# Three quarters of the sigmoid gates by seven half-block products, with the weight sums on GpSimd

## The chip, the cores and the metric

One core of one Trainium2 chip runs the whole kernel in one launch. The metric is the device time of an execution in microseconds (us), lower is better. Engines are named as in the profile: PE is TensorE, ACT is ScalarE, DVE is VectorE, POOL is GpSimd, SP is SyncE.

## The reference

Two transformer blocks in float32 on 512 tokens of width 1024. What matters here lies in the first block, behind its two attentions ya and yb (each 512 wide):

```
h = rms_norm(x, g_pre[l]);  proj = h @ w_in[l];  ..., gates = split(proj)      # gates: 2048 columns
gate_a, gate_b = split(sigmoid(gates))                                          # 1024 columns each
merged = gate_a * (ya @ w_branch[l, 0]) + gate_b * (yb @ w_branch[l, 1])
y = merged @ w_out[l];  x = x + rms_norm(y, g_post[l])
```

## The kernel before, in words

**Arithmetic.** Every float32 operand of a matrix product is split into a rounded part `hi` and a rest `lo`, and each product is three matmuls, hi·hi, hi·lo and lo·hi (`three`, L1015 to L1019). Activations are held with features on the partitions: `h_hi` and `h_lo` have 8 blocks of 128 features by 512 tokens.

**The ring of weights.** Weights come in halves of 128 x 1024 elements (512 KB). SP loads a half into one of two buffers `w_raw` (`load_half`, L725), ACT copies it rounded into `w_hi` (`split_hi`, L1667), DVE writes the rest `w_lo` (`split_lo`, L2413), and PE uses it. `w_hi` and `w_lo` have four slots; the split of half u waits until PE has done with half u-4 (`slot_free`), and the load of a half waits until the half two before it is split (`split_done`).

**The gates stage.** It follows the second attention ("diff"). The 1024 merged features are done in four quarters of 256. A quarter has four gate halves (128 gate columns each: two of branch A, two of branch B; `gate_group`, L1092, 24 matmuls of 512 columns each) and two branch halves (`branch_half`, L1126, again 24 matmuls each, 12 for ya and 12 for yb). The results go to the four banks of `lin`. ACT applies the sigmoid (L1987, into `t_g`) and splits the weights that come next, DVE multiplies the branch products by the gates (L2723), adds them (`t_c`, L2726) and writes the rest `m_lo` (L2730) beside ACT's `m_hi` (L1992). The two banks of `sc` and the two of `tr` are idle in this stage. Behind it stands the output product `out1` (L1423). Each engine runs its instructions in the order in which they are written; only semaphores tie the engines together.

POOL's work ahead of this stage is the normalising of the attention's rows (`normalise`, L837); in the stage it only issues two loads of gains (L944, L945).

## Time and profile before

| | |
|---|---|
| median of 3 runs | 1180.98 us (1180.74 to 1181.24) |
| the profiled execution, its own time | 1180.78 us |
| span of its trace | 1179.0 us |
| PE busy | 1159.6 us, 98% of the span |
| DVE, ACT, POOL busy | 63%, 53%, 14% |
| granted TensorE clock, mean | 0.998 |

The span runs from the first to the last instruction; the time has 1.8 us more around it. A busy share is an average over all stages, so what a change of one stage is worth is read from that stage's own rows.

### The profile page before, as it was taken

The numbers are of one execution on the slowest core, as the hardware profiler recorded it, in microseconds if no ns is written. First come the engines' busy times: TensorE is split into PE (matmuls) and PEld (weight loads), VectorE is DVE, ScalarE is ACT, GpSimd is POOL, SyncE is SP. The second block draws the span as 40 slices with busy tenths as digits, with TensorE's granted clock in tenths as the row PEclk, the third lists the DMA queues.
The fourth block names the chain that finished last, engine by engine and source line by source line (L and its number), as shares of the span: only waits on it lengthen the run. The fifth ranks groups of instructions, "written<-read, shape, count | busy, mean of one in ns | idle before, by whom it ended". The sixth has DMA issues, their size and how long they took to land.

```text
span 1179.0 us, 15978 instructions
## 1 busy us (share of the span) xinstructions
PE 1159.6 (98%) x5903; PEld 972.7 (83%) x5903; DVE 744.1 (63%) x1227; ACT 625.3 (53%) x1054; POOL 162.5 (14%) x253
## 2 busy tenths in 40 slices
PE   8999999899999999999999999999999999999997
PEld 7788888788888888787878898888988888888885
DVE  6667578754343386684498774464658559568578
ACT  5567786684333255533776453452465355464464
POOL 3244225400000020000133000110010000010010
PEclk9999999999999999999999999999999999999999
DMA  6422232215333552552013555131294562834632
GB/s 201 109 63 64 72 107 72 54 54 143 93 85 107 178 165 75 185 162 77 22 56 125 170 152 154 59 108 56 86 253 106 185 152 58 252 89 102 200 72 89
DMA packets 152170, 136.00 MB, mean 115 GB/s; under 512 B 5569, under 2 KB 122385, under 8 KB 152098
## 3 DMA queue, kind: packets, MB, share of 16 engines
q1 hardware_dynamic: 144688, 113.13, 31.8%
q0 software_dynamic: 4000, 13.67, 6.0%
q10 hardware_dynamic: 3410, 8.25, 1.9%
q8 instruction: 45, 0.74, 0.3%
q14 instruction: 27, 0.22, 0.1%
HBM read 118.20 MB, written 6.82 MB: 106 GB/s over the span
## 4 chain that ended last, share of the span: by engine, by line
PE 86%; DVE 7%; ACT 2%; issue 2%; DMA 2%; POOL 0%; DVEq 0%; ACTq 0%; POOLq 0%
PE lin L1017 23%; PE lin L1019 22%; PE lin L1018 22%; PE tr L1199 2%; PE sc L1019 2%; PE sc L1018 2%; PE sc L1017 2%; PE tr L1192 1%; DVE w_lo L2413 1%; PE tr L1019 1%; PE tr L1018 1%; PE tr L1017 1%; PE sc L1212 1%; PE sc L1209 1%; PE lin L1233 1%
## 5 line engine op out<-in xcount | busy, mean ns | idle before, releaser
L1017 PE MATMUL lin<-h_hi,w_hi 128*128 128x512 f32 (+1 forms) x824 | 316.4, 384 | 0.9 <-ACT g_v L1757 0.7
L1019 PE MATMUL lin<-h_hi,w_lo 128*128 128x512 f32 (+1 forms) x824 | 309.4, 375 | 0.0
L1018 PE MATMUL lin<-h_lo,w_hi 128*128 128x512 f32 (+1 forms) x824 | 309.1, 375 | 0.0
L2413 DVE TENSOR_TENSOR w_lo<-w_raw,w_hi 128x1024 fp32r<-128x1024 f32 x160 | 196.2, 1230 | 136.9 <-ACT w_hi L1667 136.1
L1667 ACT ACTIVATE w_hi<-w_raw 128x1024 fp32r<-128x1024 f32 x162 | 170.6, 1055 | 142.6 <-PE lin L1019 44.5
L1019 PEld LDWEIGHTS lin<-h_hi,w_lo 128*128 128x128 f32 x824 | 155.1, 188 | 28.5
L1017 PEld LDWEIGHTS lin<-h_hi,w_hi 128*128 128x128 f32 x824 | 155.3, 188 | 28.1 <-ACT g_v L1757 0.9
L1018 PEld LDWEIGHTS lin<-h_lo,w_hi 128*128 128x128 f32 x824 | 155.4, 189 | 24.9
L2413 DVE TENSOR_TENSOR u_lo<-u_raw,u_hi 128x256 fp32r<-128x256 f32 (+2 forms) x48 | 37.4, 779 | 70.2 <-ACT u_hi L2297 37.6
L1017 PE MATMUL lin<-w_hi,h_hi 128*128 128x512 f32 x160 | 64.0, 400 | 0.0
L1019 PE MATMUL lin<-w_hi,h_lo 128*128 128x512 f32 x160 | 62.4, 390 | 0.0
L1018 PE MATMUL lin<-w_lo,h_hi 128*128 128x512 f32 x160 | 62.4, 390 | 0.0
L1705 ACT ACTIVATE p<-p,neg_max 128x128 f32<-128x128 f32 (+1 forms) x80 | 44.8, 560 | 33.0 <-DVE neg_max L2444 32.5
L837 POOL TENSOR_SCALAR p<-p,rden 128x128 f32<-128x128 f32 (+1 forms) x80 | 47.3, 592 | 93.9 <-DVE rden L2449 93.5
L2292 ACT ACTIVATE u_raw<-lin 128x512 f32<-128x512 f32 x32 | 19.1, 596 | 71.9 <-PE lin L1019 71.9
L2274 ACT ACTIVATE w_hi<-wd_b 128x1024 fp32r<-128x1024 f32 x32 | 33.5, 1058 | 30.2 <-PE lin L1019 20.4
L1714 ACT ACTIVATE pt_hi<-tr 128x128 fp32r<-128x128 f32 (+1 forms) x80 | 34.3, 429 | 20.0 <-PE tr L1199 19.5
L2454 DVE TENSOR_TENSOR pt_lo<-tr,pt_hi 128x128 fp32r<-128x128 f32 (+1 forms) x80 | 38.5, 484 | 9.0 <-ACT pt_hi L1714 8.5
L2413 DVE TENSOR_TENSOR w_lo<-wd_b,w_hi 128x1024 fp32r<-128x1024 f32 x32 | 38.8, 1224 | 5.2 <-ACT w_hi L2274 5.2
L1199 PE MATMUL tr<-ident,p 128*128 128x128 f32 x200 | 35.6, 276 | 5.6 <-DVE pt_lo L2454 4.5
L2444 DVE CUSTOM_DVE_ANT_0 p<-sc,bias_c 128x128 f32<-128x128 f32 (+3 forms) x52 | 25.3, 487 | 24.3 <-PE sc L1212 22.7
L1017 PE MATMUL sc<-w_hi,u_hi 128*128 128x512 f32 x96 | 37.4, 390 | 0.0
(401 smaller groups left out, 2338.1 us busy)
## 6 DMA issues: line engine op xcount, KB each, us to landing
w_raw<-in_w_in SPq DMA_DIRECT2D x74, 512.0 KB, 4.0
w_raw<-in_w_up SPq DMA_DIRECT2D x32, 512.0 KB, 4.3
wd_b<-in_w_down SPq DMA_DIRECT2D x24, 512.0 KB, 5.2
w_raw<-in_w_out SPq DMA_DIRECT2D x16, 512.0 KB, 3.7
w_raw<-in_w_xkv SPq DMA_DIRECT2D x16, 512.0 KB, 3.9
x_m<-in_x SPq DMA_DIRECT2D x8, 512.0 KB, 6.3
w_raw<-in_w_branch SPq DMA_DIRECT2D x8, 512.0 KB, 3.6
w_raw<-in_w_xq SPq DMA_DIRECT2D x8, 512.0 KB, 3.6
```

The costliest lines, as they stand in the source:

```text
L837: pool.tensor_scalar(p, p, rden[:, s:s + 1], 1.0, ALU.mult, ALU.mult).then_inc(s_norm, 1)
L1017: pe.matmul(o, lh, rh, start=start, stop=False)
L1018: pe.matmul(o, lh, rl, start=False, stop=False)
L1019: return pe.matmul(o, ll, rh, start=False, stop=stop)
L1199: mm = pe.transpose(tr[:, r % 2, P * j:P * j + P], src(j), ident[:, :])
L1667: act.activation(w_hi[u % SLOTS][:, :], w_raw_of(u)[:, :], ACT.Copy).then_inc(w_hi_s, 1)
L1705: act.activation(p, x, ACT.Exp, bias=neg_max[:, s:s + 1], scale=sign, accum_out=denom[:, s:s + 1]).then_inc(s_exp, 1)
L1714: act.activation(blocks(B["pt_hi"], h % 2, i), tr[:, r % 2, 0:P * (i + 1)].rearrange("p (j c) -> p j c", c=P), ACT.Copy)\
L2274: act.activation(w_hi[u % SLOTS][:, :], wd(place, part), ACT.Copy).then_inc(w_hi_s, 1)
L2413: return dve.tensor_tensor(out, x, as_f32(hi), ALU.subtract)
L2444: dve.tensor_tensor_reduce(p, sc[:, s % 2, 0:n], bias[:, T - n:T], -1.0, 3.0e38, ALU.add, ALU.min, neg_max[:, s:s + 1]).then_inc(s_max, 1)
L2454: dve.tensor_tensor(blocks(B["pt_lo"], h % 2, i), tr[:, r % 2, 0:P * (i + 1)].rearrange("p (j c) -> p j c", c=P), as_f32(blocks(B["pt_hi"] ...
```

## The change

The first quarter of the gates stays. In the other three quarters the two gate halves of a branch form a **pair**. Its two by two blocks are the two column blocks by the two halves of the 1024 inputs (4 blocks of 128 each), the tokens are cut into two halves of 256, and the two by two product is computed by seven products of half blocks in place of eight (`gate_pair`): each is 12 matmuls of 256 columns. There are six pairs.

- **Input sums.** Four sums of half blocks of h are made once by POOL (ten additions of 128 x 1024), from the moment the last scores of the attention are done, split by ACT and DVE, and kept.
- **Weight sums.** For each pair POOL makes four sums of 128 x 512 from the two raw halves (`weight_sums`). They are split like weights, two to a slot, so a pair takes four slots: the first half, two sums, the used part of the second half, two sums. Both `w_raw` buffers stay taken until the four sums are made.
- **Products** land in quarters of the ring `sc`, `sc`, `tr`, `tr` (256 columns each). ACT copies products 1 and 6 out, DVE and POOL add up the four quarters of the result, and ACT applies the sigmoid in place.
- The loops over half of the gates, written with register offsets before, are written out.

```
+PAIR_FIRST, PAIR_SUMS_A, PAIR_SECOND, PAIR_SUMS_B = range(4)
+PAIR_ORDER = [1, 2, 4, 3, 5, 6, 7]
...
+        for part, raw, last in ((PAIR_FIRST, True, 2), (PAIR_SUMS_A, False, 4), (PAIR_SECOND, True, 5),
+                                (PAIR_SUMS_B, False, 7)):
+            self.part_of[len(self.half_last_step)] = (pair, part)
+            self.half(name, raw=raw)
+            self.half_last_step[-1] = first + last
...
-    for _ in range(4):
-        p.t_halves("gates", "A", 4)
+    for quarter in range(4):
+        if quarter == 0:
+            p.t_halves("gates", "A", 4)
+        else:
+            p.pair_products("gates")
+            p.pair_products("gates")
...
+            n = 7 * pair + PAIR_ORDER.index(product)
+            return (sc, tr)[n // 2 % 2][:, n % 2, 0:256]
...
+                    if OF_RAW[r - 2] in PLAN.part_of:
+                        sp.wait_ge(gate_sums, 4 * PLAN.part_of[OF_RAW[r - 2]][0] + 4)
...
+            pool.wait_ge(s_done, S0["diff"] + 32)
+            raw = [B["t_raw"][:, n, :, :] for n in range(4)]
+            def of_h(part, row, col):
+                return as_f32(h_block(part, row, col))
+            def h_sum(out, tmp, one, other):
+                link(pool.tensor_tensor(out, of_h("hi", *one), of_h("hi", *other), ALU.add))
+                link(pool.tensor_tensor(tmp, of_h("lo", *one), of_h("lo", *other), ALU.add))
+                pool.tensor_tensor(out, out, tmp, ALU.add).then_inc(turn_made, 1)
+            def h_added(out, x, block):
+                link(pool.tensor_tensor(out, x, of_h("hi", *block), ALU.add))
+                pool.tensor_tensor(out, out, of_h("lo", *block), ALU.add).then_inc(turn_made, 1)
+            h_sum(raw[0], raw[1], (0, 0), (0, 1))
+            pool.wait_ge(turn_made, 1)
+            h_added(raw[1], raw[0], (1, 1))
+            pool.wait_ge(turn_made, 2)
+            h_added(raw[2], raw[1], (1, 0))
+            pool.wait_ge(turn_lo, 1)
+            h_sum(raw[3], raw[0], (0, 1), (1, 1))
             pool.wait_ge(y_lo_s, 8)
             pool.dma_start(B["gain"][:, 0, :], row("g_post")).then_inc(gain_in[1], 16)
             pool.dma_start(B["gain"][:, 1, :], row("norm_mix_2")).then_inc(gain_in[2], 16)
...
+            def weight_sums(pair):
+                u = PAIR_HALF[pair]
+                raw_ready(pool, u)
+                raw_ready(pool, u + PAIR_SECOND)
+                if pair > 0:
+                    split_done(pool, PAIR_HALF[pair - 1] + PAIR_SUMS_B)
+                first, second = w_raw_of(u), w_raw_of(u + PAIR_SECOND)
+                w11, w12, w21, w22 = first[:, 0:T], first[:, T:2 * T], second[:, 0:T], second[:, T:2 * T]
+                s2, s3, s1, s4 = (B["s_raw"][:, n, :] for n in range(4))
+                pool.tensor_tensor(s3, w11, w21, ALU.add).then_inc(gate_sums, 1)
+                pool.wait_ge(gate_sums, 4 * pair + 1)
+                pool.tensor_tensor(s2, s3, w22, ALU.subtract).then_inc(gate_sums, 1)
+                pool.wait_ge(gate_sums, 4 * pair + 2)
+                pool.tensor_tensor(s1, w21, w22, ALU.subtract).then_inc(gate_sums, 1)
+                pool.wait_ge(gate_sums, 4 * pair + 3)
+                pool.tensor_tensor(s4, s2, w12, ALU.subtract).then_inc(gate_sums, 1)
+                pool.wait_ge(gate_sums, 4 * pair + 4)
...
+                pool.wait_ge(gate_copied, 2 * pair + 2)
+                pool.wait_ge(gate_out, 5 * pair + 2)
+                pool.wait_ge(dve_evac, DN[branch_groups(pair // 2, 1) + 1])
+                pool.tensor_tensor(g[:, 0, :], u2, m6, ALU.add).then_inc(gate_rest, 1)
+                pool.wait_ge(gate_out, 5 * pair + 3)
+                pool.tensor_tensor(g[:, 1, :], u3, m6, ALU.add).then_inc(gate_rest, 1)
+            weight_sums(0)
+            for pair in range(0, PAIRS, 2):
+                weight_sums(pair + 1)
+                sums_with_m6(pair)
+                sums_with_m6(pair + 1)
+                if pair + 2 < PAIRS:
+                    weight_sums(pair + 2)
...
+                for k in range(4):
+                    mm = three(pair_place(pair, product), wh[:, k0 + k, :], wl[:, k0 + k, :], xh[:, k, :], xl[:, k, :],
+                               k == 0, k == 3)
...
+            def gate_pair(pair):
+                last = pair - 1
+                if pair > 0:
+                    pe.wait_ge(gate_out, 5 * last + 3)
+                pair_product(pair, 1, PAIR_FIRST, 0, lambda part: h_block(part, 0, 0))
+                if pair > 0:
+                    pe.wait_ge(gate_out, 5 * last + 4)
+                pair_product(pair, 2, PAIR_FIRST, 4, lambda part: h_block(part, 1, 0))
+                if pair > 0:
+                    pe.wait_ge(gate_copied, 2 * last + 2)
+                pair_product(pair, 4, PAIR_SUMS_A, 0, sum_ready(pair, 4))
+                if pair > 0:
+                    pe.wait_ge(gate_out, 5 * last + 5)
+                pair_product(pair, 3, PAIR_SUMS_A, 4, sum_ready(pair, 3))
+                pe.wait_ge(gate_copied, 2 * pair + 1)
+                pair_product(pair, 5, PAIR_SECOND, 4, sum_ready(pair, 5))
+                pe.wait_ge(gate_out, 5 * pair + 1)
+                pair_product(pair, 6, PAIR_SUMS_B, 0, sum_ready(pair, 6))
+                pe.wait_ge(gate_out, 5 * pair + 2)
+                pair_product(pair, 7, PAIR_SUMS_B, 4, lambda part: h_block(part, 1, 1))
...
+                    sums = B["s_raw"][:, 0:2, :] if part == PAIR_SUMS_A else B["s_raw"][:, 2:4, :]
+                    out, x = w_hi[u % SLOTS][:, :], sums.rearrange("p a b -> p (a b)")
+                    act.wait_ge(gate_sums, 4 * pair + (2 if part == PAIR_SUMS_A else 4))
...
+            def pair_copies(pair, behind):
+                u = PAIR_HALF[pair] + SLOTS
+                if pair > 0:
+                    act.wait_ge(gate_out, 5 * (pair - 1) + 2)
+                gate_copy(pair, 1, 0)
+                behind()
+                for part in (PAIR_FIRST, PAIR_SUMS_A, PAIR_SECOND):
+                    split_hi(u + part)
+                if pair > 0:
+                    act.wait_ge(gate_rest, 2 * pair)
+                gate_copy(pair, 6, 1)
...
+            def behind_pair(pair):
+                def f():
+                    split_hi(PAIR_HALF[pair] + SLOTS + PAIR_SUMS_B)
+                    pair_sigmoids(pair)
+                return f
+            for quarter in range(1, 4):
+                first = 2 * quarter - 2
+                pair_copies(first, behind_branches(quarter - 1))
+                pair_copies(first + 1, behind_pair(first))
+                pair_sigmoids(first + 1)
+                split_hi(PAIR_HALF[first + 1] + SLOTS + PAIR_SUMS_B)
+                split_hi(gate_halves(quarter)[1][0] + SLOTS)
+                for n in range(2):
+                    merged_hi(2 * quarter + n)
...
+                pair_done(dve, pair, 2)
+                dve.wait_ge(gate_copied, 2 * pair + 1)
+                dve.tensor_tensor(g[:, 0, 0:256], m1, pair_place(pair, 2), ALU.add).then_inc(gate_out, 1)
+                pair_done(dve, pair, 4)
+                if pair > 0:
+                    dve.wait_ge(gate_rest, 2 * pair - 1)
+                dve.tensor_tensor(u2, m1, pair_place(pair, 4), ALU.subtract).then_inc(gate_out, 1)
+                split_lo(u)
+                pair_done(dve, pair, 3)
+                dve.wait_ge(gate_out, out + 2)
+                if pair > 0:
+                    dve.wait_ge(gate_rest, 2 * pair)
+                dve.tensor_tensor(u3, u2, pair_place(pair, 3), ALU.add).then_inc(gate_out, 1)
+                pair_done(dve, pair, 5)
+                dve.wait_ge(gate_out, out + 3)
+                dve.tensor_tensor(g[:, 1, 0:256], pair_place(pair, 5), u3, ALU.subtract).then_inc(gate_out, 1)
+                split_lo(u + PAIR_SUMS_A)
+                split_lo(u + PAIR_SECOND)
+                pair_done(dve, pair, 7)
+                dve.wait_ge(gate_rest, 2 * pair + 1)
+                w = g[:, 0, 256:T]
+                dve.scalar_tensor_tensor(w, pair_place(pair, 7), -1.0, w, ALU.mult, ALU.subtract).then_inc(gate_out, 1)
...
+                pair_sums(first, behind_branches_lo(quarter - 1))
+                pair_sums(first + 1, behind_pair_lo(first))
+                merge(quarter, 0)
+                behind_pair_lo(first + 1)()
+                merged_lo(2 * quarter)
+                split_lo(gate_halves(quarter)[1][0] + SLOTS)
+                merge(quarter, 1)
+                merged_lo(2 * quarter + 1)
```

**POOL, from the last row of the attention on.** Names: `t_raw` are the input sums, `s_raw` the weight sums, `g_u` copies and partial results of a pair, `t_g` the gates. Before:

```order
L940 TENSOR_SCALAR rden<-rden,neg_lam 128x1
L837 TENSOR_SCALAR p<-p,rden 128x512
L944 DMA gain<-in_g_post 128x1024
L945 DMA gain<-in_norm_mix 128x1024
L950 TENSOR_TENSOR rstd<-var,minus_half 128x1 x2
```

Now, from the fourth input sum to the end of the first pair's weight sums (seven additions of `t_raw` stand ahead of it):

```order
L1014 TENSOR_TENSOR t_raw<-h_hi 128x1024 [waits turn_lo]
L1015 TENSOR_TENSOR t_raw<-h_lo 128x1024 [waits pool_self]
L1016 TENSOR_TENSOR t_raw<-t_raw 128x1024 [waits pool_self]
L1031 DMA gain<-in_g_post 128x1024 [waits y_lo_s]
L1032 DMA gain<-in_norm_mix 128x1024
L1044 TENSOR_TENSOR s_raw<-w_raw 128x512 [waits w_loaded0,w_loaded1]
L1046 TENSOR_TENSOR s_raw<-s_raw,w_raw 128x512 [waits gate_sums]
L1048 TENSOR_TENSOR s_raw<-w_raw 128x512 [waits gate_sums]
L1050 TENSOR_TENSOR s_raw<-s_raw,w_raw 128x512 [waits gate_sums]
```

And behind the weight sums of a quarter's second pair:

```order
L1060 TENSOR_TENSOR t_g<-g_u 128x256 [waits gate_out,dve_evac,gate_copied,gate_sums]
L1062 TENSOR_TENSOR t_g<-g_u 128x256 [waits gate_out]
L1060 TENSOR_TENSOR t_g<-g_u 128x256 [waits dve_evac,gate_out,gate_copied]
L1062 TENSOR_TENSOR t_g<-g_u 128x256 [waits gate_out]
L1044 TENSOR_TENSOR s_raw<-w_raw 128x512 [waits w_lo_s,w_loaded0,w_loaded1]
```

POOL had no arithmetic here. Now the weight sums of a quarter's first pair (the last row) stand behind the additions (L1060, L1062) for the two pairs before, and those wait for ACT's copy of product 6 (`gate_copied`).

**ACT, in the gates.** Before, between the first sigmoids:

```order
L1667 ACTIVATE w_hi<-w_raw 128x1024
L1984 REGISTER_ALU
L1987 ACTIVATE t_g<-lin 128x512
L673 REGISTER_ALU
L1667 ACTIVATE w_hi<-w_raw 128x1024
```

Now, in the second pair of a quarter, from the copy of product 1 to the copy of product 6:

```order
L2160 ACTIVATE g_u<-tr 128x256 [waits lin_step,gate_out]
L1829 ACTIVATE w_hi<-s_raw 128x1024 [waits lin_step,gate_sums]
L2165 ACTIVATE t_g<-t_g 128x512 [waits gate_rest,gate_out]
L2165 ACTIVATE t_g<-t_g 128x512 [waits gate_out]
L1829 ACTIVATE w_hi<-w_raw 128x1024 [waits lin_step,w_loaded1]
L1829 ACTIVATE w_hi<-w_raw 128x1024 [waits lin_step,w_loaded0]
L1829 ACTIVATE w_hi<-w_raw 128x1024 [waits lin_step,w_loaded1]
L2160 ACTIVATE g_u<-sc 128x256 [waits lin_step,gate_rest]
```

The copy of product 6 (the last row) stands behind three splits of raw weights: two branch halves and the first half of the next quarter's first pair, each of which waits for its own load.

## Rows read from the trace of the kernel before
**Rows 1.** The page: busy time, share, instructions of each engine; shares of the chain that ended last.
```profile
PE 1159.6 (98%) x5903; PEld 972.7 (83%) x5903; DVE 744.1 (63%) x1227; ACT 625.3 (53%) x1054; POOL 162.5 (14%) x253
...
PE 86%; DVE 7%; ACT 2%; issue 2%; DMA 2%; POOL 0%; DVEq 0%; ACTq 0%; POOLq 0%
```

**Rows 2.** Busy time by stretch: us, each engine's busy time, granted clock, DMA share, GB/s.
```profile
250.60:272.40 21.80, 21.80 (x98) 18.04 (x98) 11.32 (x15) 17.75 (x23) 1.17 (x2) 1.00 0.28 80
272.40:381.20 108.80, 108.80 (x482) 90.09 (x481) 43.15 (x49) 34.60 (x42) 0.00 (x0) 1.00 0.38 105
```

**Rows 3.** Timeline of PE: first product of the gates, first of the output product.
```profile
250.60 0.39 PE L1017 MATMUL lin<-h_hi,w_hi 128*128 128x512 f32 x1
...
381.19 0.39 PE L1017 MATMUL lin<-w_hi,m_hi 128*128 128x512 f32 x1
```

**Rows 4.** Timeline of PE, 256 columns: first and last of 34 products.
```profile
442.91 0.28 PE L1017 MATMUL lin<-h_hi,w_hi 128*128 128x256 f32 x1
...
446.87 0.28 PE L1017 MATMUL lin<-h_hi,w_hi 128*128 128x256 f32 x1
```

**Rows 5.** Groups by line and shape: busy us, mean ns of one, idle before, releaser.
```profile
L929 POOL TENSOR_TENSOR t_b<-t_b,rope_s 128x512 f32<-128x512 f32 x8 | 10.4, 1295 | 37.5 <-ACT t_b L1915 25.2 <-DMA rope_s<-in_rope_sin 12.4
...
L837 POOL TENSOR_SCALAR p<-p,rden 128x512 f32<-128x512 f32 x20 | 14.9, 746 | 15.2 <-DVE rden L2449 15.2
...
L837 POOL TENSOR_SCALAR p<-p,rden 128x128 f32<-128x128 f32 x20 | 7.4, 370 | 30.7 <-DVE rden L2449 30.5
...
L1667 ACT ACTIVATE w_hi<-w_raw 128x1024 fp32r<-128x1024 f32 x162 | 170.6, 1055 | 142.6 <-PE lin L1019 44.5 <-DMA w_raw<-in_w_in 28.7 <-PE tr L1019 13.1
...
L1714 ACT ACTIVATE pt_hi<-tr 128x256 fp32r<-128x256 f32 x20 | 7.4, 370 | 1.0 <-PE tr L1199 1.0
...
L2413 DVE TENSOR_TENSOR w_lo<-w_raw,w_hi 128x1024 fp32r<-128x1024 f32 x160 | 196.2, 1230 | 136.9 <-ACT w_hi L1667 136.1
...
L2454 DVE TENSOR_TENSOR pt_lo<-tr,pt_hi 128x256 fp32r<-128x256 f32 x20 | 8.3, 416 | 2.1 <-ACT pt_hi L1714 2.1
```

**Rows 6.** Timeline of POOL and DVE, stretches in which both run.
```profile
111.18 0.61 POOL L879 CAST q_one<-q_st 64x512 fp32r<-64x512 f32 x1
...
111.37 1.50 DVE L2413 TENSOR_TENSOR w_lo<-w_raw,w_hi 128x1024 fp32r<-128x1024 f32 x1
...
191.86 0.26 POOL L940 TENSOR_SCALAR rden<-rden,neg_lam 128x1 f32<-128x1 f32 x1 [4.30 <-DVE rden L2669]
...
195.90 1.47 POOL L940 TENSOR_SCALAR rden<-rden,neg_lam 128x1 f32<-128x1 f32 x1 [1.15 <-DVE rden L2669]
...
196.10 1.22 DVE L2413 TENSOR_TENSOR w_lo<-w_raw,w_hi 128x1024 fp32r<-128x1024 f32 x1
```

**Rows 7.** SP's queue: two loads of weights, and the us to landing of each.
```profile
277.32 0.37 SPq L735 DMA_DIRECT2D w_raw<-in_w_in  x1
278.86 0.37 SPq L735 DMA_DIRECT2D w_raw<-in_w_in  x1
...
w_raw<-in_w_in SPq DMA_DIRECT2D x1, 512.0 KB, 4.1
...
w_raw<-in_w_in SPq DMA_DIRECT2D x1, 512.0 KB, 4.9
```

**Rows 8.** Timeline of POOL and ACT before and at the gates.
```profile
233.02 0.69 POOL L837 TENSOR_SCALAR p<-p,rden 128x512 f32<-128x512 f32 x1
...
266.70 0.62 POOL L944 DMA_DIRECT2D gain<-in_g_post  x1 [32.98 <-DVE y_lo L2413]
267.33 0.55 POOL L945 DMA_DIRECT2D gain<-in_norm_mix  x1
...
265.97 0.60 ACT L1987 ACTIVATE t_g<-lin 128x512 f32<-128x512 f32 x1
...
274.76 1.06 ACT L1667 ACTIVATE w_hi<-w_raw 128x1024 fp32r<-128x1024 f32 x1 [5.32 <-DMA w_raw<-in_w_in]
```

More of the change, by code:

```diff
@@ L1090, in head_sum, with pair_product @@
                 pe.matmul(sum_bank(h), ones_r[:, :], lo, start=False, stop=True).then_inc(sum_t, 1)
-            def gate_group(u, g, first, off):
-                if first is not None:
-                    pe.wait_ge(act_evac, AN[g - 4] + off.act)
-                    pe.wait_ge(dve_evac, DN[G["gates"][0] - 1] - 3 + first + off.dve)
-                else:
-                    claim(g, off)
-                split_done(pe, u, off)
+            def pair_product(pair, product, part, k0, x):
+                u = PAIR_HALF[pair] + part
+                split_done(pe, u)
@@ new lines, in _ @@
+            for n in range(4):
+                g = G["gates"][n]
+                step(g)
+                act.wait_ge(dve_evac, DN[G["gates"][0] - 1])
+                act.activation(B["t_g"][:, n, :], bank(g), ACT.Sigmoid).then_inc(act_evac, 1)
+                if n < 3:
+                    next_hi("gates", n)
+                if n > 0:
+                    turned_sum_hi(n - 1)
+            turned_sum_hi(3)
+            merged_hi(0)
+            for n in range(3, 5):
+                next_hi("gates", n)
@@ new lines, in _ @@
+            for quarter in range(1, 4):
[5 more added lines that the diff above has]
+                split_hi(gate_halves(quarter)[1][0] + SLOTS)
+                for n in range(2):
+                    merged_hi(2 * quarter + n)
+            behind_branches(3)()
@@ new lines, in _, with behind_branches_lo @@
+            for n in range(4):
+                if n < 3:
+                    next_lo("gates", n)
+                if n > 0:
+                    turned_sum_lo(n - 1)
+            merge(0, 0)
+            turned_sum_lo(3)
+            merged_lo(0)
+            for n in range(3, 5):
+                next_lo("gates", n)
+            merge(0, 1)
+            merged_lo(1)
+            def behind_branches_lo(quarter):
+                return lambda: next_lo("gates", 5) if quarter == 0 else split_lo(gate_halves(quarter)[1][1] + SLOTS)
@@ new lines, in behind_pair_lo @@
+            def behind_pair_lo(pair):
+                return lambda: split_lo(PAIR_HALF[pair] + SLOTS + PAIR_SUMS_B)
+            for quarter in range(1, 4):
+                first = 2 * quarter - 2
+                pair_sums(first, behind_branches_lo(quarter - 1))
[6 more added lines that the diff above has]
+                merged_lo(2 * quarter + 1)
```

201 lines of the change are left out of this document (140 added, 61 removed).

## The prediction

> **What bounds the kernel now.** The page comes first [rows 1]: PE is busy 98% of the span, and the chain that ended last is 86% PE, so whatever PE is spared, or is made to wait, shows in the time. The table by stretch [rows 2] says the same of the gates: in both stretches PE is busy for the whole stretch at granted clock 1.00, DVE for 52% and 40% of it, and POOL does next to nothing. The timeline of PE gives the pace [rows 3]: the stage's 576 matmuls of 512 columns fill 381.19 - 250.60 = 130.6 us, 0.2267 us each. There is no wait to remove here; the change must pay through fewer columns, and it must not make PE wait.
>
> The sum is made against the profiled execution, 1180.78 us (span 1179.0), which lies 0.2 us below the median of 1180.98.
>
> **What PE is spared.** A pair was 48 matmuls of 512 columns, 48 x 0.2267 = 10.88 us. Now it is 7 x 12 = 84 of 256 columns. Their pace is in the stage behind the output product [rows 4]: (446.87 - 442.91) / 33 = 0.120 us, which is more than half of 0.2267, so a pair takes 10.08 us. Six pairs save 6 x 0.80 = **4.8 us**. The results go to banks that nothing else uses here, and the sigmoids only move; they cost PE nothing.
>
> **What POOL gets.** Prices first [rows 5]. An addition of 128 x 512 takes 1.29 us, and 1.34 with the wait for its own result. For 128 x 1024 no row exists. Twice 1.29 = 2.59 is the upper bound. For the lower one the fixed part is taken from POOL's `tensor_scalar`, 746 ns for 512 columns against 370 for 128, or 0.245 at no columns; the rest, 1.05, doubled gives 2.35. I take 2.37, and 0.77 for 256 columns. The Trainium skill has a figure for the same operation (GPSIMD Engine Reference, section 3.1): 4497 ns for 2048 columns. By that and the row's 1.29 an estimate would be 2.36, and the sum would stay.
>
> The second price is that of running beside DVE. In the first example of [rows 6] DVE's `w_lo` starts at 111.37 while POOL's cast runs until 111.79, and takes 1.50 us in place of 1.23. In the second, POOL's operation on one column starts at 195.90 and takes 1.47 in place of 0.26: it ends at 197.37, 0.05 after DVE's `w_lo` (196.10 to 197.32). So a DVE instruction that reads two tensors in SBUF and a POOL one that reads SBUF exclude each other, and the later waits for nearly all of the other. The Trainium skill states it as an exclusive lock on a shared read interface that is held for the whole instruction (SBUF — State Buffer, section "Who interferes with whom"). If the lock held for `tensor_scalar` and casts alone, as the rows have it, the sum below would lose its waits; by the page's rule they stand, additions included. Every split `w_lo`, every `t_c` and every `m_lo` is such a DVE instruction, and now every weight sum is such a POOL one. Bounds for the excluded time: nothing at all (rival one), or the full wait at each meeting. I take the full wait, since both directions are in the rows.
>
> **Where it ends up: the first pair.** POOL is free at 233.7 [rows 8]. Seven of the ten additions take 7 x 2.42 = 17 us and, with DVE's splits between, end near 258. The last three wait for the first input sum to be split, which stands behind ACT's first two sigmoids and splits (from 265.97) and DVE's: about 270.9. Three additions are 7.3 us, with 3.1 us of meetings (DVE has four such instructions there): 281.3. The two gain loads, 0.62 and 0.55 us of issue, now stand behind them: 282.5. Four weight sums are 5.4 us, plus 2.7 of meetings: all made at 290.6, the first two at 286.4. PE reaches the first pair at 283.2 and product 4 at 286.1, but the first slot of sums has ACT's 1.06 and DVE's 1.23 to go [rows 5]: 288.8. The copy of product 1, behind the late merge, costs 0.7 more, and the first DVE sum (product 6 waits for it) 1.1: about 4.2 us in the first pair.
>
> **The ring.** Both `w_raw` buffers are held until a pair's four sums are made. Two loads that start close together land 4.1 and 6.5 us after the first issue: issued at 277.32 and 278.86, they land at 281.4 and 283.8, so the second comes 2.4 behind the first [rows 7]. From the sums of a quarter's second pair to those of the next quarter's second pair, one after the other:
> - branch half loaded 4.1; split, 1.06 + 1.23 + 0.1 = 2.4 (its `w_lo` frees the buffer); next pair's first half loaded 4.1;
> - its split on ACT and, behind it, the copy of product 6, 1.06 + 0.37 = 1.4;
> - POOL's two additions of 256 columns 1.6, with 0.75 of meeting DVE's `w_lo` of the same half;
> - four weight sums 5.4, with 2.3 of meetings (two splits and `m_lo`);
> - both loads of the second pair 6.5; its four weight sums 5.4, with 1.4 of meetings.
>
> That is **35.2 us** (30.8 without the 4.4 us of meetings). PE's work for a quarter is 2 x 10.08 + 48 x 0.2267 = 31.0 us. So the ring, not PE, sets the pace: PE waits 4.1 us in each quarter, in my walk 1.1 us at product 6 of the first pair, 1.3 at product 4 and 1.6 at product 3 of the second.
>
> **Sum.** All sums of pair 0 at 290.6; of pair 1 at 290.6 + 6.5 + 5.4 + 1.3 = 303.8; two turns of the ring, 374.2. From the last weight sum to the output product: POOL's addition, DVE's last sum and their waits 1.4, then products 3, 5, 6, 7 at 1.44 = 5.8, and the branch halves 10.9: 18.0 in all. The output product starts at 392.2 in place of 381.2, **11.0 us later**. Counted the other way, 4.2 + 2.9 in the first quarter, 4.1 in each of the two others, 0.6 at the end of the attention, where a split is held up by an addition, make 15.9 of waits, against 4.8 spared: 11.1. Behind the stage nothing changes, and PE has no slack there to make it up. Forecast: 1180.8 + 11.0 = **1191.8 us**.
>
> Costed at nothing: DVE's and ACT's added work (the input sums' splits, five small DVE sums a pair). DVE was idle for half of the stretch; without that cover each would add its own 0.4 to 1.2 us to the turn of a pair.
>
> **Rival one, faster.** Additions on POOL and DVE's splits do not exclude each other. Then the ring turns in 30.8 us, 0.2 under PE's 31.0, no wait is left, and the time is 1180.8 - 4.8 = 1176.0. For it: POOL's additions in [rows 5] take 1.29 us in all eight cases, none with such a DVE instruction running before it. Against it: [rows 6]. Were each load 0.4 us slower, the ring would be the longer by half a microsecond, and the time up to 1178.4. It decides at ring = 31.0: below, it is faster.
>
> **Rival two, partly hidden.** Meetings cost half of what I walked: ring 33, waits 2 a quarter, the first pair 3 us: 1180 to 1186, around 1183.5. For it: DVE's splits may fall between POOL's sums, since POOL waits some 6 us for the loads in each pair.
>
> **Rival three, the attention's end pays too.** DVE's four `t_lo` before the head sums read two tensors in SBUF, and PE waits for them. If POOL's long additions get in between them, each is held up by over 2 us, PE waits there for about 6 us before the gates begin. The first pair then waits less, but the ring is the same: 1192 to 1198. Against it: instructions of DVE that follow one another without a gap keep POOL out.
>
> **Rival four, no gain in columns.** If the 256-column matmuls ran slower with sums as operands, each 0.01 us would add 5 us. [Rows 4] is the same operation and shape, so I give it nothing of its own.
>
> **Numbers.** Forecast (1186 to 1195) 0.60; rival one 0.18; rival two 0.15, a third of it within 0.2% of before; rival three or later 0.07. A measurement of this kernel tells 0.2%, 2.4 us, from no change, so faster means under 1178.6. The range from 1177.5 to 1196 leaves out most of rival one and the end of rival three. Faster 0.18, same 0.06, slower 0.76.
>
> **What would show it.** Right: PE idle in four to six groups ahead of products 4, 3 and 6, released by `w_lo` of sums and by DVE's small sums; POOL's 128 x 512 additions with a mean well above 1.29 us; some DVE `w_lo` of 1.5 to 2.5 us; three quarters spaced about 35 us. Wrong: POOL's additions at 1.29 throughout and PE without gaps (rival one); gaps at the head sums (three); matmuls of 256 columns spaced by more than 0.120 us (four).

## The result, and the profile after the change

The changed kernel takes **1195.7 us** (median of 4 runs, 1194.7 to 1197.0) against 1181.1 (1180.7 to 1181.2) before: a ratio of 1.0125, 95% interval 1.0107 to 1.0142, slower by 14.6 us. The profiled execution took 1194.7 us, span 1192.9; against the 1180.78 and 1179.0 of before that is 13.9 more in the span, and this is the figure that the rows below have to explain.

The page of the changed kernel, its busy times and the chain that ended last [rows 1 before]:

```profile
PE 1160.5 (97%) x6119; PEld 981.3 (82%) x6119; DVE 797.7 (67%) x1273; ACT 641.2 (54%) x1081; POOL 242.9 (20%) x299
...
PE 59%; DVE 5%; ACT 1%; issue 1%; DMA 1%; POOL 0%; DVEq 0%; ACTq 0%; POOLq 0%
```

POOL has 80 us more work, DVE 54, ACT 16. The chain is PE for 59% where it was 86%: there are new places at which PE waits. PE's busy time did not fall, although the products have fewer columns. In the quarters below it counts 32.25, 31.95 and 31.94 us for matmuls that take 31.06 us without a wait (experiment 2), so a busy time can hide a part of the waits; they are read from the timeline.

The table by stretch of the changed kernel (us, each engine's busy time, granted clock, DMA share, GB/s): the end of the attention, the head sums with the first products, the products with full blocks, and the three quarters with pairs, each from its first branch product to the next one's [rows 2]:

```profile
250.00:255.70 5.70, 0.00 (x0) 0.01 (x1) 5.70 (x4) 2.42 (x3) 3.82 (x2) 0.70 0.01 1
255.70:262.00 6.30, 6.28 (x21) 5.11 (x22) 2.82 (x4) 4.63 (x7) 0.00 (x0) 0.73 0.57 166
259.21:281.00 21.79, 21.79 (x98) 18.02 (x96) 12.43 (x16) 17.86 (x22) 3.81 (x2) 1.00 0.27 73
...
281.00:316.77 35.77, 32.25 (x217) 29.42 (x216) 30.14 (x30) 13.96 (x19) 21.45 (x14) 1.00 0.33 90
316.77:350.72 33.95, 31.95 (x218) 29.37 (x217) 23.12 (x29) 13.84 (x20) 17.35 (x12) 1.00 0.36 94
350.72:384.74 34.02, 31.94 (x219) 29.37 (x217) 23.45 (x29) 13.85 (x20) 17.33 (x12) 1.00 0.35 94
```

The timeline of PE: the first head sum, the first product of the gates [rows 3], three products that wait, and the first of the output product (start, duration, in brackets the idle time before and what ended it):

```profile
255.72 0.77 PE L1214 MATMUL sc<-t_hi,ones_r 128*128 128x512 f32 x1 [6.46 <-DVE t_lo L2658]
...
259.21 0.39 PE L1142 MATMUL lin<-h_hi,w_hi 128*128 128x512 f32 x1
...
296.10 0.36 PE L1142 MATMUL tr<-w_t,w_hi 128*128 128x256 f32 x1 [1.19 <-DVE w_lo L2658]
...
302.01 0.39 PE L1142 MATMUL sc<-w_t,w_hi 128*128 128x256 f32 x1 [0.84 <-DVE t_g L2988]
...
310.92 0.39 PE L1142 MATMUL tr<-h_hi,w_hi 128*128 128x256 f32 x1 [1.05 <-DVE t_g L3007]
...
395.64 0.39 PE L1142 MATMUL lin<-w_hi,m_hi 128*128 128x512 f32 x1
```

The output product starts at 395.64 where it started at 381.19. This trace is already 0.45 us behind at 232.8, so 14.0 us are lost between the two, in two places:

- **Before the gates, 8.2 us.** PE waits 6.46 us for DVE's first `t_lo`, in all the first head sum starts 7.1 us late (255.72, against 248.15 before and the 0.45); and the granted clock has fallen, so that the eight matmuls of the head sums take 3.5 us (255.72 to 259.21) where they took 2.45. From 262 on the clock is full again.
- **In the quarters, 5.8 us.** 35.77 + 33.95 + 34.02 = 103.7 us for three quarters that took 3 x 32.65 before. The matmuls of a quarter alone are 31.06 (an experiment below has them without a wait), so PE loses 4.7, 2.9 and 3.0 us, and is spared 3 x 1.6.

The timelines of POOL and of DVE at the end of the attention show the first place, with DVE's `y_lo` of the kernel before as the last row:

```profile
239.41 3.26 POOL L1016 TENSOR_TENSOR t_raw<-t_raw 128x1024 f32<-128x1024 f32 x1
242.75 2.81 POOL L1020 TENSOR_TENSOR t_raw<-t_raw,h_hi 128x1024 f32<-128x1024 f32 x1
245.64 2.73 POOL L1021 TENSOR_TENSOR t_raw<-t_raw,h_lo 128x1024 f32<-128x1024 f32 x1
248.45 2.70 POOL L1020 TENSOR_TENSOR t_raw<-t_raw,h_hi 128x1024 f32<-128x1024 f32 x1
251.22 2.67 POOL L1021 TENSOR_TENSOR t_raw<-t_raw,h_lo 128x1024 f32<-128x1024 f32 x1
```

```profile
240.34 1.14 DVE L2699 TENSOR_TENSOR pt_lo<-tr,pt_hi 128x384 fp32r<-128x384 f32 x2
242.59 9.10 DVE L2658 TENSOR_TENSOR y_lo<-y,y_hi 128x512 fp32r<-128x512 f32 x4 [1.11 <-ACT y_hi L2119]
251.62 3.35 DVE L2658 TENSOR_TENSOR w_lo<-w_raw,w_hi 128x1024 fp32r<-128x1024 f32 x1
254.90 2.48 DVE L2658 TENSOR_TENSOR t_lo<-t_sq,t_hi 128x512 fp32r<-128x512 f32 x4
...
242.13 2.50 DVE L2413 TENSOR_TENSOR y_lo<-y,y_hi 128x512 fp32r<-128x512 f32 x4 [2.23 <-ACT y_hi L1957]
```

Four `y_lo` take 9.10 us; before they took 2.50. The `w_lo` behind them takes 3.35 in place of 1.23. The two engines take turns: one POOL addition, one DVE instruction, one POOL addition. The first `y_lo` takes 0.69 us, as before, and the longest of the other three 2.91. The additions pay 0.3 to 0.4 each (2.67 to 2.81 against the 2.39 of the first), the `y_lo` 6.6 together and the `w_lo` 2.1, and `t_lo`, on which PE waits, stands behind the four additions that start at 242.75 to 251.22. `pt_lo`, which reads `tr` in PSUM and only one tensor in SBUF, took 1.14 us beside an addition and 1.15 before: it was not held up. What the additions cost DVE ahead of the `y_lo` (a `w_lo` of 2.33 us, for one) fell into time in which DVE had been idle.

POOL's groups by line and shape (count | busy us, mean ns of one | idle before) show the second place; 1.29 us was the price of a 128x512 addition [rows 5]:

```profile
L1050 POOL TENSOR_TENSOR s_raw<-s_raw,w_raw 128x512 f32<-128x512 f32 x6 | 12.9, 2151 | 0.5
...
L1046 POOL TENSOR_TENSOR s_raw<-s_raw,w_raw 128x512 f32<-128x512 f32 x6 | 11.2, 1874 | 0.5
...
L1048 POOL TENSOR_TENSOR s_raw<-w_raw 128x512 f32<-128x512 f32 x6 | 9.3, 1556 | 0.5
L1044 POOL TENSOR_TENSOR s_raw<-w_raw 128x512 f32<-128x512 f32 x6 | 7.7, 1291 | 20.7 <-DVE w_lo L2658 20.7
```

The same operation takes 1.29 us where it comes first (L1044) and up to 2.15 where DVE's splits fall upon it.

### The profile page after: what moved, and what is told of

Same layout as the page of the kernel before. It is cut to its first block, busy times and chain, and to the rows that moved or that the text cites. A ratio compares the mean times of both kernels' runs of the same rounds, so it can differ in the third digit from the quotient of the medians.

```text
span 1192.9 us, 16364 instructions
## 1 busy us (share of the span) xinstructions
PE 1160.5 (97%) x6119; PEld 981.3 (82%) x6119; DVE 797.7 (67%) x1273; ACT 641.2 (54%) x1081; POOL 242.9 (20%) x299
## 4 chain that ended last, share of the span: by engine, by line
PE 59%; DVE 5%; ACT 1%; issue 1%; DMA 1%; POOL 0%; DVEq 0%; ACTq 0%; POOLq 0%
PE lin L1142 15%; PE lin L1144 15%; PE lin L1143 15%; PE sc L1143 2%; PE sc L1144 2%; PE sc L1142 2%; PE tr L1342 1%; PE tr L1142 1%; PE tr L1143 1%; PE tr L1144 1%; PE tr L1349 1%; DVE w_lo L2658 1%; DMA wd_b<-wd_a 1%; PE sc L1632 1%; PE tr L1632 1%
## 5 line engine op out<-in xcount | busy, mean ns | idle before, releaser
L1142 PE MATMUL lin<-h_hi,w_hi 128*128 128x512 f32 (+1 forms) x728 | 279.0, 383 | 0.8 <-ACT g_v L1919 0.6
L1144 PE MATMUL lin<-h_hi,w_lo 128*128 128x512 f32 (+1 forms) x728 | 272.0, 374 | 0.0
L2658 DVE TENSOR_TENSOR w_lo<-w_raw,w_hi 128x1024 fp32r<-128x1024 f32 (+1 forms) x160 | 204.4, 1278 | 101.1 <-ACT w_hi L1829 100.3
L1143 PE MATMUL lin<-h_lo,w_hi 128*128 128x512 f32 (+1 forms) x728 | 271.8, 373 | 0.0
L1829 ACT ACTIVATE w_hi<-w_raw 128x1024 fp32r<-128x1024 f32 (+1 forms) x162 | 167.9, 1039 | 119.7 <-PE lin L1144 27.2
L1142 PEld LDWEIGHTS lin<-h_hi,w_hi 128*128 128x128 f32 x728 | 137.4, 189 | 24.3 <-ACT g_v L1919 0.8
L1144 PEld LDWEIGHTS lin<-h_hi,w_lo 128*128 128x128 f32 x728 | 137.1, 188 | 24.7
L1143 PEld LDWEIGHTS lin<-h_lo,w_hi 128*128 128x128 f32 x728 | 137.4, 189 | 21.1
L1876 ACT ACTIVATE pt_hi<-tr 128x128 fp32r<-128x128 f32 (+1 forms) x80 | 34.4, 429 | 20.0 <-PE tr L1349 19.5
L1113 POOL DMA_DIRECT2D wd_b<-wd_b x8 | 7.1, 881 | 177.9 <-DVE wd_t L3482 177.9
```

Source lines behind the costliest of these rows:

```text
L1142: pe.matmul(o, lh, rh, start=start, stop=False)
L1143: pe.matmul(o, lh, rl, start=False, stop=False)
L1144: return pe.matmul(o, ll, rh, start=False, stop=stop)
L1829: act.activation(out, x, ACT.Copy).then_inc(w_hi_s, 1)
L1876: act.activation(blocks(B["pt_hi"], h % 2, i), tr[:, r % 2, 0:P * (i + 1)].rearrange("p (j c) -> p j c", c=P), ACT.Copy)\
L2658: return dve.tensor_tensor(out, x, as_f32(hi), ALU.subtract)
```

## The experiments

**Theory A**: POOL instructions that read SBUF and DVE instructions with two inputs in SBUF hold each other back, and both losses come from that. **Theory B**: the waits come from the order of the work, or from its mere length. The first four kernels leave each engine's work in place and time, and take away only what POOL reads.

**1. Input sums only written**.

```
-   link(pool.tensor_tensor(out, x, of_h("hi", *block), ALU.add))
+   link(pool.memset(out, 1.0)); link(pool.memset(out, 1.0)); link(pool.memset(out[:, 0, :], 1.0))
    (so for each of the ten additions)
```

> The input sums are left out: in place of each 128x1024 addition GpSimd writes constants into the same buffer for as long (two memsets of 128x1024 and one of 128x256, about 2.4 us), which read nothing. Theory A (GpSimd's reads and VectorE's instructions on two SBUF inputs hold each other back, and this made the 6.5 us wait before the head sums): no VectorE instruction between 234 and 258 is longer than in the kernel before (w_lo 1.23, four y_lo 2.5), the head sums start near 249.3 in place of 255.7, TensorE's clock stays up, 1195.7 - 8.2 = 1187.5 us; the waits in the pairs stay (quarters of 34 to 35.5 us). Theory B (the wait comes from the order of the work or from GpSimd's time, not from what it reads): 1195 to 1196 us, the wait stays.

Measured: **1187.97 us** (1186.85 to 1188.84), 7.7 us less than the changed kernel. POOL is as busy as before between 234 and 251, with memsets of 0.96, 0.96 and 0.31 us; DVE and PE of that kernel in the same stretch:

```profile
242.90 2.50 DVE L2665 TENSOR_TENSOR y_lo<-y,y_hi 128x512 fp32r<-128x512 f32 x4 [2.23 <-ACT y_hi L2126]
245.89 1.23 DVE L2665 TENSOR_TENSOR w_lo<-w_raw,w_hi 128x1024 fp32r<-128x1024 f32 x1 [0.50 <-ACT w_hi L1836]
```

```profile
248.91 0.39 PE L1221 MATMUL sc<-t_hi,ones_r 128*128 128x512 f32 x1
```

The four `y_lo` are back at 2.50, `w_lo` at 1.23, the head sums start without a wait. The quarters stay at 36.0, 34.3 and 34.1 us. That is 0.5 us above theory A's number, and B's is out: it is what the additions read, not the time they fill.

**2. Weight sums only written**.

```
-   pool.tensor_tensor(s3, w11, w21, ALU.add).then_inc(gate_sums, 1)
+   written_sum(s3).then_inc(gate_sums, 1)      (and so s2, s1, s4)
```

> The weight sums are left out: GpSimd writes constants in place of each addition for as long (memsets of 128x512, 128x512 and 128x64, about 1.3 us). Theory A: the 6.5 us before the head sums stay, the quarters of pairs fall from 35.8, 34.0, 34.0 to about 31.2 each (TensorE's own work is 31.0), 1195.7 - 9.5 = about 1186.5 us. Theory B (the quarters are stretched by the chain of copies and sums between the products, or by GpSimd's own time, which is the same here): quarters of 34 us stay, 1194 to 1196 us.

Measured: **1185.5 us** (1185.0 to 1186.2), 10.2 less. The wait of 6.46 us at the head sums is unchanged. The three quarters in the table by stretch of this kernel:

```profile
281.29:312.51 31.22, 31.22 (x218) 29.21 (x217) 24.97 (x29) 14.08 (x19) 17.17 (x30) 1.00 0.38 104
312.51:343.57 31.06, 31.06 (x219) 29.17 (x218) 19.88 (x29) 13.85 (x20) 13.23 (x28) 1.00 0.41 103
343.57:374.63 31.06, 31.06 (x219) 29.17 (x218) 19.72 (x29) 13.94 (x20) 13.23 (x28) 1.00 0.39 102
```

PE is busy from end to end of each: the ring without its meetings is under PE's 31.06 us.

**3. Both only written**: the two edits together.

> Input sums and weight sums both replaced by writes of the same length. Theory A: both losses go, 1195.7 - 8.2 - 9.5 = 1178.0 us, faster than the kernel before by about 3 us; the product saving of 4.8 us shows nearly whole. Theory B: 1194 to 1196 us.

Measured: **1177.2 us** (1176.7 to 1177.6), ratio to the kernel before 0.9967 (0.9955 to 0.9980). 18.5 us less than the changed kernel, where the two alone gave 7.7 + 10.2 = 17.9: within 0.6 us the losses are separate and add up. Of the 4.8 us that the seven products spare PE, 3.8 arrive: the quarters take 31.5, 31.2 and 31.1 us, 93.8 in all against 97.9 before.

**4. PE kept busy in its wait**.

```
+   for n in range(27):
+       pe.matmul(bank(G["gates"][0]), ones_r[:, :], hh[:, 0, :], start=True, stop=True)
    for h in range(4):
        head_sum(h, B["t_hi"][:, h, :], B["t_lo"][:, h, :], 0)
```

> 27 matmuls of 512 columns into a free bank stand ahead of the four head sums, about as long as TensorE's wait there (6.1 us at full clock). Theory A (the wait costs 6.5 us itself, and 1.6 us more because the clock is down for the 21 matmuls behind it): head sums start at the same time, 255.7, the clock stays at full, the gates start 1.6 us earlier, 1194.1 us. Rival: the slower matmuls behind the wait have another cause, 1195.7 us, or the filling matmuls delay the head sums, 1196 to 1197 us.

Measured: **1195.65 us** (1194.5 to 1198.3), the changed kernel's time. A miss for theory A's number, though the mechanism shows in PE's timeline and in the first row of POOL's last three input sums:

```profile
248.80 6.28 PE L1566 MATMUL lin<-h_hi,ones_r 128*128 128x512 f32 x27
255.43 0.50 PE L1214 MATMUL sc<-t_hi,ones_r 128*128 128x512 f32 x1 [0.35 <-DVE t_lo L2661]
...
257.81 0.39 PE L1142 MATMUL lin<-h_hi,w_hi 128*128 128x512 f32 x1
```

```profile
275.71 2.41 POOL L1014 TENSOR_TENSOR t_raw<-h_hi 128x1024 f32<-128x1024 f32 x1 [22.02 <-DVE w_t L2661]
```

The granted clock is 1.00 throughout, the gates start 1.4 us earlier, and POOL's additions too (275.71 against 277.11). But the output product starts at 395.07 against 395.64: the three quarters take 36.2, 34.4 and 34.1 us in place of 35.8, 33.95 and 34.0 and use more than half of the gain up again; nothing of it is left in the time. So the slow clock at the head sums cost nothing that this edit could get back by itself; why the quarters grew is not shown. The rival had the right number for another reason: it expected the slower matmuls to stay or the head sums to come late, and neither happened.

**5. Input sums on DVE**: in its idle places, the lo parts added one after the other without a second buffer.

```
+   if w == 18:
+       dve.wait_ge(s_done, S0["diff"] + 32)
+       h_add(0, 2)                        # two of the ten additions
...
    if w == 22:
+       h_add(2, 4)
        for k in range(4): split_y(k, k)
...
    next_lo("zb", 3)
+   h_add(4, 8)
    head_norms(0, B["y_1"], lambda h: B["t_sq"][:, h, :])
+   h_add(8, 10)
```

> The ten input sums are on VectorE, in its idle places (two after each of its last waits on the scores, four behind the last t_lo, two before the gated y), the weight sums stay on GpSimd. Theory A (GpSimd's reads against VectorE's two-input instructions, both losses apart): the 6.5 us before the head sums go, each addition takes 1.2 us, the quarters of pairs stay at 34 to 35, out1 starts near 387, 1187.5 us (1186.5 to 1189.5). Theory B (the additions cost VectorE what the exclusion cost, whoever makes them): the head sums still start late by about 5 us or more, 1192 us or more.

Measured: **1187.67 us** (1187.3 to 1188.3), as theory A has it. DVE needs 1.22 us for what takes POOL 2.39 at best, the four `y_lo` take 2.50 again, and `t_lo` is not late:

```profile
241.08 1.23 DVE L2916 TENSOR_TENSOR t_raw<-t_raw,h_hi 128x1024 f32<-128x1024 f32 x1
242.34 2.50 DVE L2634 TENSOR_TENSOR y_lo<-y,y_hi 128x512 fp32r<-128x512 f32 x4
```

**6. Weight sums on DVE**.

```
+   if pair % 2 == 0:
+       weight_sums(pair + 1)              # with dve in place of pool
    split_lo(u + PAIR_SUMS_A)
...
+   if quarter < 3:
+       weight_sums(2 * quarter)
    merge(quarter, 0)
```

> The four weight sums of each pair are on VectorE (0.7 us each, 17 us in all), the input sums stay on GpSimd. Theory A: the wait before the head sums stays at 6.5 us, the quarters fall to about 33 (first) and 31.8 (second and third), 1190 us (1188.5 to 1191.5). Theory B (VectorE's own time in a quarter is the bound, so that more work there stretches it): quarters of 35 us and more, 1196 us or more.

Measured: **1190.3 us** (1189.4 to 1190.9). The wait at the head sums stays at 6.46 us; the quarters are 34.60, 31.68 and 31.67 us. 17 us more work on DVE cost little: in the second quarter DVE is busy for 80% and PE for 99% of the time, and the quarter is 0.6 us longer than the 31.06 without a wait. Theory B is out here too.

**7. Both on DVE**: the two edits together.

> Input and weight sums both on VectorE, placed as in the two kernels that move one of them. Theory A: neither loss is left, quarters of 34.1, 31.9, 31.8 us, 1180.5 to 1181.5 us, level with the kernel before: the saving of 4.8 us is spent on waits of the first quarter (product 4 for its sums, 0.7; product 5 and 6, 1.8) and 0.7 a quarter behind. Theory B: over 1185 us.

Measured: **1183.2 us** (1182.6 to 1184.2, 11 runs), ratio 1.0016 (1.0007 to 1.0025). Both losses are gone, but this is 2 us above what I expected. PE waits 2.71 us at product 4 of the first pair in place of 0.7.

**8. Both on DVE, and another order**.

```
    # ScalarE, first quarter
+   next_hi("gates", 3)
    turned_sum_hi(3)
    merged_hi(0)
...
    # VectorE, first quarter
    weight_sums(0)
+   next_lo("gates", 3)
    merge(0, 0)
...
    # ScalarE, pair_copies
    gate_copy(pair, 1, 0)
+   if pair == 0:
+       merged_hi(1)
    behind()
    for part in (PAIR_FIRST, PAIR_SUMS_A, PAIR_SECOND):
+       if part == PAIR_SECOND and pair % 2 == 1:
+           gate_copy(pair, 6, 1)          # product 6 ahead of the split
        split_hi(u + part)
```

> As the kernel with both on VectorE, and the order changed on two engines: the sums' half of the first pair is split before the first merge, the second merged block's copy stands behind the copy of product 1, VectorE's first sum of the pair ahead of the next split, and in each second pair of a quarter product 6 is copied ahead of the last split. Theory A (what is left of the waits is the order of ScalarE's and VectorE's rows): quarters of 33.2, 31.1, 31.0 us, 1178.5 us (1177.5 to 1179.5), faster than the kernel before by 0.2%. Rival (the waits come from something else, such as a load or a semaphore's own time): 1180.5 to 1181.5 us as without the order.

Measured: **1181.5 us** (1180.5 to 1182.3, 11 runs), ratio 1.0003 (0.9994 to 1.0012): level with the kernel before, 3 us above the expectation. Two quarters run at 31.06 us; in the first a wait of 3.12 us is left before product 6. The rows of ACT and POOL show a cause that I had not counted:

```profile
275.55 1.06 ACT L1782 ACTIVATE w_hi<-w_raw 128x1024 fp32r<-128x1024 f32 x1 [4.57 <-DMA w_raw<-in_w_in]
```

```profile
267.31 0.62 POOL L1007 DMA_DIRECT2D gain<-in_g_post  x1 [33.56 <-DVE y_lo L2616]
```

The two gain rows, 1 MB, are loaded as soon as the last `y_lo` is done, at 267. That is where the kernel before had them too, at 266.70, and ACT waited 5.32 us for a load there [rows 8], but with no pair's product behind it. In the changed kernel POOL's additions kept them back until 285. Here they share the DMA engines with the weight half that ACT needs.

**9. The same, gains loaded later**.

```
-   pool.wait_ge(y_lo_s, 8)                # and the two dma_start of "gain"
...
    sums_with_m6(pair + 1)
+   if pair == 0:
+       pool.dma_start(B["gain"][:, 0, :], row("g_post")).then_inc(gain_in[1], 16)
+       pool.dma_start(B["gain"][:, 1, :], row("norm_mix_2")).then_inc(gain_in[2], 16)
```

> As the kernel with both on VectorE and the order changed, and the two gain rows are loaded after the first two pairs' sums of GpSimd (near 310) in place of right behind the last y_lo (267). Theory C (what the order did not give was a transfer: the weight half that ScalarE waited 4.6 us for until 275.6 shared the DMA engines with the gains' 1 MB): that half is split near 273.4, the wait of 3.1 us before product 6 of the first pair falls to about 1.5, 1179.7 us (1178.8 to 1180.6). Rival (VectorE's rows alone set that wait): the half lands no earlier or the wait stays, 1181.5 us.

Measured: **1178.7 us** (1178.5 to 1180.8, 11 runs), ratio 0.9982 (0.9973 to 0.9991). First the DMA issues between 262 and 280 of the kernel with the early gains, then ACT's row, and the issues in the same stretch, of this one (KB each, median us from issue to landing):

```profile
w_raw<-in_w_in SPq DMA_DIRECT2D x2, 512.0 KB, 6.8
...
gain<-in_norm_mix POOLq DMA_DIRECT2D x1, 512.0 KB, 5.8
```

```profile
273.81 1.06 ACT L1782 ACTIVATE w_hi<-w_raw 128x1024 fp32r<-128x1024 f32 x1 [2.37 <-DMA w_raw<-in_w_in]
```

```profile
w_raw<-in_w_in SPq DMA_DIRECT2D x2, 512.0 KB, 4.2
```

The two weight loads land after 4.2 us in the median in place of 6.8, and the wait before product 6 is 1.49 us in place of 3.12. Theory C holds; the time is 0.1 us under its range.

**10. And the first pair's rows put ahead of the merged blocks**.

```
    turned_sum_lo(3)                       # VectorE, first quarter
    next_lo("gates", 4)
    merge(0, 0)
    merge(0, 1)
...                                        # merged_lo(0), merged_lo(1): between the sums of pair 0
```

> As that kernel, and in the first pair VectorE's and ScalarE's rows on which the products wait stand ahead of the merged blocks' halves: the last input sum's half and the second half block ahead of both merges, both merges ahead of the pair's first sum, the m_lo behind its second and third sum. Theory C: no wait over 1 us is left in the pairs, quarters of 31.3, 31.0, 31.0 us, 1177 to 1178.5 us, faster than the kernel before by 0.2 to 0.3%. Rival (VectorE has no room in the first quarter, so that a wait removed there comes back at the next product): 1179.5 to 1181 us.

Measured: **1176.9 us** (1176.6 to 1177.1, 5 runs), ratio 0.9965 (0.9951 to 0.9978): faster than the kernel before by 4.2 us, with everything computed, and level with the kernel in which POOL only writes in place of the input and weight sums (1177.2). Its quarters, by stretch:

```profile
273.03:304.49 31.46, 31.26 (x218) 29.21 (x216) 28.40 (x38) 16.13 (x22) 3.20 (x3) 1.00 0.36 92
304.49:335.55 31.06, 31.06 (x219) 29.17 (x217) 25.46 (x36) 13.95 (x20) 5.55 (x7) 1.00 0.51 138
335.55:366.61 31.06, 31.06 (x219) 29.17 (x217) 24.41 (x36) 13.72 (x20) 3.39 (x4) 1.00 0.40 107
```

DVE is busy for 28.4 of 31.5 us in the first one: 3.1 us are left there.

**11. POOL begins later**: the changed kernel, but the input sums start behind the fourth `t_lo`.

```
-   pool.wait_ge(s_done, S0["diff"] + 32)
+   pool.wait_ge(sq_lo, 4)
```

> As the changed kernel, but GpSimd begins the input sums when VectorE's fourth t_lo is done (about 250) and not at the last scores (234). Theory A: no wait before the head sums and the clock stays up, but the additions now meet VectorE's w_lo, head norms and y, which end 7 us later, so that TensorE waits about 4 us for y_lo at the first branches and 5 to 7 us at product 4 of the first pair: 1198 to 1200 us, slower than the changed kernel. Rival (the loss at the attention's end is a matter of that place alone): 1187.5 to 1189 us.

Measured: **1198.4 us** (1198.2 to 1200.0), slower than the changed kernel by 2.7 us. The head sums start in time, at 248.31. Then the additions meet the head norms and the gating on DVE, and PE waits behind those:

```profile
256.56 10.88 DVE L2763 TENSOR_TENSOR y<-y,t_sq 128x512 f32<-128x512 f32 x4 [2.85 <-ACT t_sq L1937]
267.47 4.76 DVE L2953 SCALAR_TENSOR_TENSOR y<-y,g_subln,z_b 128x512 f32<-128x512 f32 x4
```

```profile
277.11 0.47 PE L1142 MATMUL lin<-y_hi,w_hi 128*128 128x512 f32 x1 [4.38 <-DVE w_lo L2658]
298.60 0.55 PE L1142 MATMUL tr<-w_t,w_hi 128*128 128x256 f32 x1 [5.85 <-DVE w_lo L2658]
```

Four operations of 0.6 us each take 10.88 us. In both places tried, POOL's 17 us of additions meet such DVE instructions; to begin at the last scores, as the change does, is the better of the two.

**12. Product 6 copied ahead of the split**: the changed kernel, weight sums on POOL, and only the edit to `pair_copies` that copies product 6 ahead of the split (shown under 8).

> The changed kernel with one row moved: in the second pair of each quarter ScalarE copies product 6 ahead of the split of the next half block (near 316) and not behind it (320.3), where that split waits for its load. GpSimd's two additions with product 6 then no longer stand ahead of the weight sums of the next pair. Ring theory (what sets the quarters is the chain load, sum, split, product that hands a buffer back, and the two additions, 2.2 us, lie on it where their copy is late): quarters two and three shorten by 1.0 to 1.7 us each, 1193 us (1192 to 1194). Rival (the quarters are set by the meetings of GpSimd and VectorE alone, wherever the rows stand): 1195 to 1196 us.

Measured: **1192.6 us** (1190.8 to 1195.2), about 3 us less than the changed kernel and in the range of the ring theory; the quarters of the profiled execution, the fastest of the four, are 34.28, 32.31 and 32.72 us in place of 35.77, 33.95 and 34.02. In the changed kernel the turn of the ring shows in these rows of ACT and POOL:

```profile
319.28 1.06 ACT L1829 ACTIVATE w_hi<-w_raw 128x1024 fp32r<-128x1024 f32 x1 [3.40 <-DMA w_raw<-in_w_in]
320.25 0.37 ACT L2160 ACTIVATE g_u<-sc 128x256 f32<-128x256 f32 x1
```

```profile
320.69 1.50 POOL L1060 TENSOR_TENSOR t_g<-g_u 128x256 f32<-128x256 f32 x1 [9.68 <-DMA w_raw<-in_w_in]
...
322.85 1.29 POOL L1044 TENSOR_TENSOR s_raw<-w_raw 128x512 f32<-128x512 f32 x1
```

and in this one:

```profile
315.27 1.78 POOL L1060 TENSOR_TENSOR t_g<-g_u 128x256 f32<-128x256 f32 x1 [5.05 <-ACT g_u L2160]
...
320.49 1.32 POOL L1044 TENSOR_TENSOR s_raw<-w_raw 128x512 f32<-128x512 f32 x1 [2.75 <-issue]
```

The copy waited behind a split that waited for its load, and with it the two additions, and behind them the next pair's weight sums; they now start 2.4 us earlier (320.49 against 322.85), although the gates of this execution took 1 us longer. So the quarters are set by a ring, and the meetings are one part of its length, the order another. What an execution of this kernel takes spreads over 4.4 us, and the slowest of the four lies within the changed kernel's own range. The 1 us is the clock's: the gates' first products took 22.8 us in place of 21.8, with a granted clock of 0.50 over 255.00 to 260.00.

## Why the prediction was right, and where it was not

The sign and the range were right: slower, 1195.7 us, in 1177.5 to 1196. There was luck in it. The forecast of 1191.8 was 3.9 us short, the result lies 0.3 us inside the range's upper end and just outside the forecast's own (1186 to 1195), in that of rival three, to which I gave 0.07. And three terms missed in part against each other: the attention's end by 7.6 us too little, the first quarter by 2.4 too much, the other two by 1.2 and 1.1 too much. The mechanism, exclusion and the ring of loads, sums and splits, was the right one; it also acted where I had ruled it out.

- **What PE is spared, 4.8 us: right.** 31.06 us a quarter with no wait in it (experiments 2 and 10), as computed (31.0), and 32.65 before.
- **POOL's prices: right.** The first 128x1024 addition takes 2.39 us (2.37 taken), 128x512 1.29, 128x256 0.73 (0.77 taken).
- **The exclusion: right, additions included.** It was worked out from casts and `tensor_scalar` [rows 6]. Experiments 1 and 2 add that a POOL instruction that only writes does not take part. The Trainium skill states the rule with that limit (SBUF — State Buffer, "Who interferes with whom"): a VectorE instruction with two SBUF inputs contends with a GpSimd one that reads SBUF, not with one that only writes it. By that rule, the traces agree: `y_lo` x4 9.10 us against reads, 2.50 against writes.
- **The ring: right, a little long.** From the sums of pair 1 (309.19) to those of pair 3 (343.16) it turned in 34.0 us; forecast 35.2. The meetings in that turn, each POOL row against its undisturbed one, come to 3.9 us (forecast 4.4), and the rest is 30.1 (30.8). PE's waits in the second and third quarter are 2.9 and 3.0 us, forecast 4.1 each. The longest stood at product 6 of the first pair and product 3 of the second, as walked, but hardly any at product 4 of the second. My terms of the ring add up to 35.35, not 35.2, and those of the first pair (2.7, 0.7 and 1.1) to 4.5, not 4.2; neither changes the outcome. In rival one, loads 0.4 us slower, at least three to a turn, make the ring about 1 us longer than PE's work, not half a microsecond.
- **The first quarter: too large a term.** 4.2 + 2.9 = 7.1 forecast, 4.7 found. PE came 8.2 us late to it, and POOL only some 4 us later than in my walk (the first pair's sums done at 294.2, forecast 290.6).
- **The end of the attention: this step failed.** "0.6 at the end of the attention, where a split is held up by an addition": found 8.2 us. What failed is the argument that I set against rival three, "instructions of DVE that follow one another without a gap keep POOL out". They do not: DVE's four `y_lo` follow without a gap, and an addition comes between each two (9.10 us for 2.50). With [rows 6] I had seen single meetings only, and took from them that who is there first goes first; an engine that is already waiting goes before the other's next instruction. The rows add up: the `y_lo` cost 6.6 us more and the `w_lo` 2.1, less the 0.5 that DVE was idle between them before and the 1.2 that the first `t_lo` had in hand (done at 246.96, used at 248.15): 7.0, and the first head sum is 7.1 late. The slow clock adds the rest of the 8.2. Rival three had the place, the wait (about 6 us) and the time; it named the `t_lo`, but the instructions held up were those ahead of them.
- **Numbers.** 8.2 + 4.7 + 2.9 + 3.0 = 18.8 of waits against 3 x 1.6 spared give 14.0; my other count had 15.9 against 4.8. The signs of the forecast were found (quarters near 34 us, 128x512 additions of 1.71 us in the mean of all 24, against 1.29), and so was that of rival three, the gap at the head sums.
- **DVE's and ACT's added work, costed at nothing: right for its length.** With 24.4 and 25.5 us of DVE work the second and third of the three quarters of experiment 10 run at 31.06.
- **Rival one** (no exclusion, 1176.0) is what experiment 3 made: 1177.2. Its time was right; its condition is not that of the chip.

Open: why the clock stays down for longer in some executions behind the head sums. No run was made for it.

## What to carry to other kernels

Before work is moved to GpSimd, list what VectorE does in that stretch. Here, wherever both had work, VectorE instructions with two inputs in SBUF took turns with GpSimd ones that read SBUF, so that a short one (0.69 us) came to take 2.9 us, even where VectorE had a queue without gaps. Where VectorE has room, the same additions belong there: they take half the time (1.22 us against 2.39), and the only GpSimd instructions left to meet them are few: in experiment 10 its twelve additions of 128x256, which still take 0.73 to 1.51 us. When an engine is emptied, look at what it issues next: here two loads moved forward by 18 us, back to where they had stood before the change, but now in the way of a load on the critical path, and cost 2.8 us.
